# The query products of a decoder's first attention layer on operands of 512 columns, with the halves added on VectorE

## What is computed

```python
h = rmsnorm(x, mixer_norm[0])
parts = split_cols(h @ even_w_in[0], [ATTN_W] * N_DIL + [ATTN_W, ATTN_W, CROSS_WIDTH])
mix = mixer_dilated(parts[:N_DIL], parts[N_DIL], parts[N_DIL + 1], rel_bias)
...
def mixer_dilated(q_groups, k, v, rel_bias):
    branches = [dilated_branch(heads(qg), kh, vh, rel_bias, w, d)
                for qg, (w, d) in zip(q_groups, DIL_PAIRS)]
    m_max = jnp.max(jnp.stack([b[1] for b in branches]), axis=0)
    ...
    return (num / den[..., None]).astype(k.dtype).reshape(B, S, ATTN_W)
```

## Time and profile before

| | |
|---|---|
| median of 3 runs | 1565.93 us (1565.57 to 1566.80) |
| the profiled execution, its own time | 1565.14 us |
| its span in the trace | 1563.4 us |
| mean granted clock of TensorE | 0.993 |
| TensorE busy | 1527.9 us (98%), 8155 matmuls |
| VectorE busy | 1326.0 us (85%) |
| ScalarE busy | 1130.7 us (72%) |
| the chain that ended last, by engine | TensorE 89%, VectorE 4%, ScalarE 3%, DMA 2% |

### The profile page before, as it was taken

The page is one execution under the profiler, slowest core; times in us unless marked ns, Lnnn a source line. Parts: engine busy times, 40 slices in busy tenths (PEclk is TensorE's granted clock), DMA queues, the critical chain, the costliest instruction groups (busy, mean ns, idle before and its releaser), DMA issues.

```text
span 1563.4 us, 25330 instructions
## 1 busy us (share of the span) xinstructions
PE 1527.9 (98%) x8155; PEld 1288.0 (82%) x8155; DVE 1326.0 (85%) x1806; ACT 1130.7 (72%) x1507; POOL 87.7 (6%) x64
## 2 busy tenths in 40 slices
PE   8899999999999999999999999999999999999997
PEld 7899977888888777888888888888888888888886
DVE  5778868777758878998998998998998998998997
ACT  5565556444446668788878878878878878878875
POOL 1333100000010000000000000000000000000000
PEclk9999999999999999999999999999999999999999
DMA  9844526666623467999999999999999999999992
GB/s 271 216 135 142 159 91 201 189 187 184 167 58 85 145 250 285 409 386 375 381 396 357 396 390 355 393 389 354 390 394 354 388 392 356 392 393 349 404 386 107
DMA packets 226997, 455.38 MB, mean 291 GB/s; under 512 B 12848, under 2 KB 120512, under 8 KB 226944
## 3 DMA queue, kind: packets, MB, share of 16 engines
q1 hardware_dynamic: 222800, 439.52, 77.7%
q0 software_dynamic: 4144, 15.22, 3.9%
HBM read 445.52 MB, written 9.18 MB: 291 GB/s over the span
## 4 chain that ended last, share of the span: by engine, by line
PE 89%; DVE 4%; ACT 3%; DMA 2%; issue 1%; POOL 0%; ACTq 0%; DVEq 0%; POOLq 0%
PE ps L733 25%; PE ps L735 25%; PE ps L734 25%; PE ps L980 5%; PE ps L982 2%; PE ps L1140 2%; DMA big<-in_even_w_in 2%; PE ps L821 1%; ACT w_hi L1178 1%; PE ps L851 1%; DVE w_lo L1525 1%; DVE small L1612 1%; PE ps L836 1%; DVE z L1590 1%; DVE z L1609 1%
## 5 line engine op out<-in xcount | busy, mean ns | idle before, releaser
L1525 DVE TENSOR_TENSOR w_lo<-big,w_hi 128x1024 fp32r<-128x1024 f32 x837 | 983.8, 1214 | 145.2 <-ACT w_hi L1178 69.6
L1438 ACT CAST w_hi<-big 128x1024 fp32r<-128x1024 f32 x672 | 693.6, 1056 | 139.6 <-PE ps L735 136.5
L733 PE MATMUL ps<-w_hi,m_hi 128*128 128x512 f32 (+1 forms) x1008 | 391.9, 389 | 1.5 <-ACT qT L1233 1.3
L735 PE MATMUL ps<-w_hi,m_lo 128*128 128x512 f32 (+1 forms) x1008 | 389.4, 386 | 0.0
L734 PE MATMUL ps<-w_lo,m_hi 128*128 128x512 f32 (+1 forms) x1008 | 389.2, 386 | 0.0
L733 PEld LDWEIGHTS ps<-w_hi,m_hi 128*128 128x128 f32 x1008 | 189.7, 188 | 41.2 <-issue 2.1
L735 PEld LDWEIGHTS ps<-w_hi,m_lo 128*128 128x128 f32 x1008 | 189.6, 188 | 38.3
L734 PEld LDWEIGHTS ps<-w_lo,m_hi 128*128 128x128 f32 x1008 | 189.7, 188 | 37.2
L1178 ACT CAST w_hi<-big 128x1024 fp32r<-128x1024 f32 (+1 forms) x171 | 165.9, 981 | 49.3 <-PE ps L735 36.8
L733 PE MATMUL ps<-w_hi,h_two 128*128 128x512 f32 (+1 forms) x464 | 182.6, 394 | 0.0
L735 PE MATMUL ps<-w_hi,h_two 128*128 128x512 f32 (+1 forms) x464 | 179.9, 388 | 0.0
(11 more groups left out here) (270 smaller groups left out, 1576.0 us busy)
## 6 DMA issues: line engine op xcount, KB each, us to landing
big<-in_odd_w_gate SPq DMA_DIRECT2D x112, 1024.0 KB, 7.3
big<-in_odd_w_up SPq DMA_DIRECT2D x112, 1024.0 KB, 7.4
big<-in_odd_w_down SPq DMA_DIRECT2D x112, 1024.0 KB, 7.5
big<-in_even_w_in SPq DMA_DIRECT2D x42, 512.0 KB, 4.0
big<-in_even_w_gate SPq DMA_DIRECT2D x22, 512.0 KB, 4.6
big<-in_even_w_up SPq DMA_DIRECT2D x22, 512.0 KB, 3.9
big<-in_even_w_down SPq DMA_DIRECT2D x22, 512.0 KB, 4.7
big<-in_w_out SPq DMA_DIRECT2D x20, 512.0 KB, 3.6
```

What stands on the lines that cost most here:

```text
L733: mm(dst, a[0], b[0], start=start, stop=False, **kw)
L735: return mm(dst, a[1], b[0], start=False, stop=stop, **kw)
L1438: nc.scalar.copy(w_hi[:, slot, :], ring[s][:, (u % 2) * UNIT:(u % 2 + 1) * UNIT]).then_inc(s_hi, 1)
L1525: return V.tensor_tensor(dst, src, lead.bitcast(F32), ALU.subtract)
```

## The change

The 24 query products (m < NBR in the first layer) become wide products. For each chunk one matmul of 512 columns takes the weights' high part by the tokens' high and low parts together, and one of 256 adds the weights' low part by the tokens' high part to the first half. The function for it, `wide_product`, is the dense layer's code taken out, and the dense layer now calls it. Keys, values and the cross pairs stay as they were. The bank then holds two halves that have to be added: ScalarE copies the second half into `half`, a view of the tile XH with two places, and raises `query_half_copied`; VectorE adds it to the first half in PSUM, writes qT and raises `evacuated` (`halves`). `evacuated` of layer 0 counts query products alone now; keys, values and the cross pairs' queries have semaphores of their own. A product's wait for its bank is therefore for VectorE's add where the bank held queries (`even_bank`), and the scores wait for the keys' copy and for the third add. On VectorE an add stands ahead of the first split, of the second split and of the third split in a step, and at the start of the stage behind pair 0's five splits.

```diff
@@ -372,6 +372,7 @@
         ysb = z[:, 0:D]
+        half = XH[:, 0, 0:2 * SEQ].rearrange("p (r n) -> p r n", r=2)
         fin_gain = qiT[:, :, :].rearrange("p c n -> p (c n)")
@@ -407,10 +408,11 @@
         s_hi, s_lo, s_used = map(sem, ("unit_hi", "unit_lo", "unit_used"))
-        names = ("evacuated", "turned_v", "values", "scores", "scores_read", "masked", "max", "exp",
+        names = ("evacuated", "cross_queries", "turned_v", "values", "scores", "scores_read", "masked", "max", "exp",
                  "added", "summed", "third_left", "third_read", "probs", "probs_turned", "probsT", "mixed", "mix_hi", "mix_lo", "dve_rden")
...
         s_me = sem("mem_evacuated")
+        s_two, s_keyT, s_valT = map(sem, ("query_half_copied", "even_keys_copied", "even_values_copied"))
         s_plo = sem("unit_lo_by_pool")
@@ -501,6 +503,10 @@
 
+        def wide_before(pair, m):
+            return pair.value(lambda g: NBR * g + m)
         def width(pair, m):
@@ -778,10 +784,39 @@
 
+            def wide_product(dst, w, norm=None):
+                for k in range(DC):
+                    if norm is not None:
+                        pe.wait_ge(s_nlo, DC * norm + k + 1)
+                    mm(dst, w[0][:, k, :], h_two[:, k, :, :].rearrange("p s n -> p (s n)"),
+                       start=k == 0, stop=k == DC - 1, skip_group_check=True)
+                    last = mm(dst[:, 0:SEQ], w[1][:, k, :], h_hi[:, k, :], start=False, stop=k == DC - 1,
+                              skip_group_check=True)
+                last.then_inc(s_used, 1)
+            def even_bank(pair, m):
+                if m == 0:
+                    pe.wait_ge(s_keyT, pair.g)
+                elif m == 1:
+                    pe.wait_ge(s_valT, pair.g)
+                else:
+                    pe.wait_ge(s_at[0]["evacuated"], wide_before(pair, m - 2) + 1)
             def project(pair, m, norm=None):
...
                 n = pair.before() + m
-                if not (isinstance(n, int) and n < 2):
+                if pair.kind == "even":
+                    if not (isinstance(n, int) and n < 2):
+                        even_bank(pair, m)
+                elif pair.cross and pair.l == 0:
+                    pe.wait_ge(S["evacuated"], NBR * PAIRS)
+                    pe.wait_ge(s_keyT, PAIRS)
+                    pe.wait_ge(s_valT, PAIRS)
+                elif pair.cross:
+                    pe.wait_ge(S["evacuated"], 3 * PAIRS)
+                elif not (isinstance(n, int) and n < 2):
                     pe.wait_ge(S["evacuated"], n - 1)
@@ -789,11 +824,17 @@
                 w = split(pair.idx, pair.span[0], pair.unit(m), kc, width(pair, m))
+                if pair.kind == "even" and m < pair.nbr:
+                    wide_product(ps[:, pair.bank(m), :], w, norm)
+                    return
                 product(ps[:, pair.bank(m), 0:SEQ], w, src, kc, norm)
...
                 S = s_at[pair.l]
-                pe.wait_ge(S["evacuated"], pair.before() + pair.mats)
+                if pair.kind == "even":
+                    pe.wait_ge(s_valT, pair.g + 1)
+                else:
+                    pe.wait_ge(S["evacuated"], pair.before() + pair.mats)
                 for t in range(TT):
@@ -804,7 +845,13 @@
                 S = s_at[pair.l]
-                pe.wait_ge(S["evacuated"], pair.before() + (1 if pair.cross else pair.nbr + 1))
+                if pair.cross:
+                    pe.wait_ge(S["cross_queries"], pair.g - PAIRS + 1)
+                elif pair.kind == "even":
+                    pe.wait_ge(s_keyT, pair.g + 1)
+                    pe.wait_ge(S["evacuated"], wide_before(pair, NBR - 1) + 1)
+                else:
+                    pe.wait_ge(S["evacuated"], pair.before() + pair.nbr + 1)
 
@@ -856,7 +903,7 @@
                 if ch == 0:
-                    pe.wait_ge(s_at[l]["evacuated"], pair_at(l, NPAIR - 1).before() + 1)
+                    pe.wait_ge(s_at[l]["cross_queries"], XPAIRS)
                     pe.wait_ge(s_at[l]["scores_read"], 2 * PAIRS + 1)
@@ -974,14 +1021,7 @@
                 bank = (4 if kind == "gate" else 6) + par
-                for k in range(DC):
-                    if norm is not None:
-                        pe.wait_ge(s_nlo, DC * norm + k + 1)
-                    mm(ps[:, bank, :], w[0][:, k, :], h_two[:, k, :, :].rearrange("p s n -> p (s n)"),
-                       start=k == 0, stop=k == DC - 1, skip_group_check=True)
-                    last = mm(ps[:, bank, 0:SEQ], w[1][:, k, :], h_hi[:, k, :], start=False, stop=k == DC - 1,
-                              skip_group_check=True)
-                last.then_inc(s_used, 1)
+                wide_product(ps[:, bank, :], w, norm)
 
@@ -1223,6 +1263,12 @@
                 act.wait_ge(s_used, along(pair.idx, pair.span[0], [u + 1 for u in pair.unit(m)]))
+                if pair.kind == "even" and m < pair.nbr:
+                    n = wide_before(pair, m)
+                    if not (isinstance(n, int) and n < 2):
+                        act.wait_ge(S["evacuated"], n - 1)
+                    nc.scalar.copy(half[:, (pair.par + m) % 2, :], ps[:, pair.bank(m), SEQ:2 * SEQ]).then_inc(s_two, 1)
+                    return
                 if pair.gs[0] == NPAIR - 1:
@@ -1230,7 +1276,11 @@
                 dst = qT[:, pair.par, m, :] if m < pair.nbr else kT[:, pair.par, :] if m == pair.nbr else vT[:, :]
-                nc.scalar.copy(dst, ps[:, pair.bank(m), 0:SEQ]).then_inc(S["evacuated"], 1)
+                if pair.kind == "even":
+                    done = s_keyT if m == pair.nbr else s_valT
+                else:
+                    done = S["cross_queries" if pair.cross else "evacuated"]
+                nc.scalar.copy(dst, ps[:, pair.bank(m), 0:SEQ]).then_inc(done, 1)
 
@@ -1612,6 +1662,15 @@
 
+            def halves(pair, m):
+                S = s_at[0]
+                dve.wait_ge(s_two, wide_before(pair, m) + 1)
+                if not (isinstance(pair.g, int) and pair.g < 2):
+                    dve.wait_ge(S["mixed"], 2 * pair.g - 1)
+                V.tensor_tensor(qT[:, pair.par, m, :], half[:, (pair.par + m) % 2, :], ps[:, pair.bank(m), 0:SEQ],
+                                ALU.add).then_inc(S["evacuated"], 1)
             def head_probs(pair, hh):
@@ -1643,10 +1702,16 @@
                     outs(lo_now, now, m)
+                def add(m):
+                    if now.gs[-1] < LATE:
+                        halves(nxt, m)
                 if now.kind == "even":
+                    add(0)
                     low(0)
+                    add(1)
                     low(1)
                     head_probs(now, 1)
+                    add(2)
                     low(2)
@@ -1678,7 +1743,10 @@
                         lo_mat(pair_at(l, 0), m)
+                    halves(pair_at(l, 0), 0)
                     for m in range(pair_at(l, 1).mats):
+                        if m + 1 < NBR:
+                            halves(pair_at(l, 0), m + 1)
                         lo_mat(pair_at(l, 1), m)
```

## The result

The changed kernel takes 1571.28 us (median of 7 runs, 1570.07 to 1574.53) beside 1565.93 for the kernel before in the same comparison (7 runs, 1565.16 to 1567.1). The ratio is **1.0043, with a 95% interval of 1.0033 to 1.0052**: slower by 0.43%. The forecast was 1568.7, at most 1570.5, and "same" as the likeliest.

What follows compares the result with a forecast made beforehand. TensorE's pace of starting matmuls was taken as the bound. Stall +2.73, clock +1.35, first step +0.06 and -0.07, six further steps -1.26 sum to +2.8 us: 1565.93 becomes 1568.7, range 1566.0 to 1570.5.

Steps and rivals of the forecast that it cites:

- What bounds the kernel: First layer's attention: TensorE's pace of starting matmuls sets the time; VectorE has some 7 us free in 40.
- Part 1, the wide products: First layer's 24 query products: fewer matmul starts gain 0.07 us a product, -1.26 us over six loop steps.
- The rival of the weight loads: Query products: time falls with their weight loads, 0.96 us a product, giving 1546.9 us; chance 0.02.
- Part 2, the adds: VectorE's 24 adds of 0.42 us: nothing lost in the loop's further steps, +0.06 us in the first step.
- Part 3, the stall: Stage start: pair 0's product 2 waits for add 0 behind the fifth unit's split, +2.80 us, net +2.73.
- Part 4, the clock: Stage start: after the new 2.85 us idle time TensorE's clock falls once more, +1.35 us (bounds 0 and 1.36).
- The slower rival: Loop: scores wait for add 2, so the steps' gains are lost; +4.2 us, 1570.1 us; 0.16 for slower in all.
- The range: Whole kernel: 1566.0 to 1570.5 us, leaving out no stall, weight loads and a tip of the slower case.

Runs made afterwards that it cites:

- experiment 2: The changed kernel with GpSimd's mask sums in the loop also waiting for the fourth split of their step: 1567.86 us, 1.0018.
- experiment 1: The changed kernel with a step's third add ahead of the second head's probabilities, not behind them: 1570.06 us, 1.0028.
- experiments 3 and 6: experiment 3, and the kernel before with only GpSimd's mask sums waiting for the fourth split of their step: 1564.32 us, 0.9990.
- experiment 9: The kernel before with ScalarE's copy of pair 0's product 0 also waiting for pair 0's last split: 1569.5 us, 1.0026.
- experiment 5: The changed kernel with 12 matmuls that nothing reads ahead of pair 0's product 2: 1571.42 us, 1.0036.
- experiment 3: The kernel before with an unused 0.41 us VectorE maximum between second probabilities and third split in each step: 1569.86 us, 1.0031.
- the cures: The changed kernel with GpSimd's sums behind the fourth split, and with copies and adds interleaved among pair 0's casts and splits: together 1565.51 us, 0.9997.

## Why the prediction was wrong

- **What bounds the kernel: right for the kernel before, and it held only there.** VectorE's "some 7 us free in 40" was an average. It did not lie behind the probabilities, where the price arose.
- **Part 1, the wide products: right for the product, half for the loop.** Query products have a chunk pitch of 0.35 (131.27, 131.62 in a step), and 0.08 a product comes out where TensorE sets the pace (experiment 2's last steps). The term was to be 1.26 in the loop; with the splits cured, the profiles show 0.7 to 0.8 over six steps, since in the middle steps TensorE waits a little for other engines. The rival of the weight loads is gone: a third fewer loads for these products, and nothing like 23 us. The busy share of the weight loads fell from 37.41 of 40 to 33.30, and the stage became longer. What the prediction's rival drew from "Perfetto Trace Analysis" of the Trainium skill (Identifying the Most-Contended Engine) is an inference that goes further than the page: it names the matmuls' share of peak work beside the busy share of the weight loads, as measures of headroom, and does not say that a product's time falls with its loads.
- **Part 2, the adds: their duration right (0.41 against 0.42), the step behind add 2 wrong.** This is the step that failed: "Behind add 2 VectorE's next split is 0.4 us later, and the one after it waits for a cast that ends later still, so the reading of the scores does not move." I moved the split and left its duration at 1.22. It became 2.29, the next one 2.2, and the reading moved by 1.4 us a step. The sentence after it, "GpSimd waits for the probabilities, not for the adds", was true, and was the cause: GpSimd's start stayed where it was while the split moved behind it. The prediction had no term for VectorE's splits in the loop, and in place of -1.26 the steps gave +2.58, an error of 3.8 us, which is more than the sum that was forecast. The earlier trace rows showed splits of 2.3 us beside mask sums, and I used it for the start alone; the earlier trace rows showed a sum of 2.27 that had waited, the other half of the same contest.
- **Part 3, the stall: the mechanism right, the size right where product 1 starts as before.** There (experiment 1) product 2 comes 2.83 us later (2.80 forecast). In the changed kernel's own profile the wait is 5.63 long, because product 1 was early, and product 2 starts 1.22 us later than before. What the prediction left out is that an early product 1 makes a wait ahead of product 2 in the kernel before as well: 3.83 and 4.30 us in the profiles of experiments 3 and 6. The stall is longer with the add, not new.
- **Part 4, the clock: not as forecast.** A second fall, on top of the one before product 1, was to cost 1.35. Only experiment 1 has two (behind 47.99 and behind 54.98), and there the parts add up: 2.83 for the stall and 1.57 for product 2 at the lower clock make the 4.39 by which its first keys come late; 4.1 was forecast. The changed kernel's own profile has one fall, as the kernel before has, only a product later: it costs product 2 2.05 us and product 1 nothing, and the first keys come 3.26 later. That the start as a whole lost about what was forecast (3.2 us by the means above, 0.26% in experiment 9) owes something to luck: three of four profiles with the start of before have a fall too, and the second fall that was forecast came in one of three with the changed start. That the clock is part of the loss over many executions is not shown (experiment 5).
- **The slower rival** had 0.16 and the wrong mechanism: no scores waited for add 2. In the changed kernel's step they are released by the keys' copy, as forecast. Its time, 1570.1, was the nearest, by chance.
- **The range** (to 1570.5) missed the median by 0.8 us. Its bounds were those of the terms that I had; a bound for a split that turns slow (1.07 us more each, two a step, against the earlier trace rows) was missing. Its chance of "slower", 0.22, was to be 0.16 and 0.07, which is 0.23; nothing hangs on it.

Left open: why the loss of 0.31% in experiment 3 is larger than the 2.6 us of its steps. Its profile has a fall of the clock at the end of the stage as well (51.41 us for 49.81); with a start 0.6 us later the three make up the 4.9 us by which its span is longer. Where this place was left as it is, the clock fell in five of seven profiles with wide products and in one of four with narrow ones, this one, and it cost 1.6 to 3.1 us (51.36 to 52.89 for 49.8). Whether late VectorE work makes that fall more likely, or chance did, one profile a kernel can't tell. So part of the change's 0.43% may lie there too; the cures leave little room for it, since with both of them the ratio is 0.9997 and that kernel's profile has the fall as well (52.89).

## What to carry to other kernels

Before putting a short operation on an engine, look at who is released by the instruction ahead of it. If another engine's work starts there and contends with the instruction behind, the insertion hands over the first place: 0.41 us cost a split of 1.22 another 1.07, twice a step, though the engine had slack on average. What cured it here is one wait that keeps the engine without urgency (here GpSimd, idle 14 us a step) behind the urgent one. And at the start of a stage count where in a queue of long operations the new one stands, not how long it takes.

## What the runs showed of the hardware

- **Two engines that hold each other off over SBUF.** A split (two operands and a result in SBUF) takes 1.22 us alone and 2.1 to 2.3 beside GpSimd's sums; a sum takes 1.27 when it comes first, 2.08 when it comes second to a split, 1294 ns on average when kept apart. VectorE's 128x256 operations that read PSUM are not held: the reading at 123.23 took 0.41 while GpSimd was in its sums (118.75 to 124.5). The page "SBUF — State Buffer" of the Trainium skill, named above, says that a VectorE operation with two SBUF inputs is concerned where GpSimd's operation reads SBUF, and that whoever starts first has the ports for the whole instruction. The traces agree: the engine that came second took about 0.8 to 1.1 us longer. Here a lead of 0.05 us was enough to be first (118.75 against 118.80, and 115.89 against 115.94 in experiment 3).
- **The same idle time, and two outcomes for the clock.** 2.41 and 2.42 us before the same matmul, at 1.00 behind one and 0.50 behind the other, with no difference in the program there. Such falls made 1.6 to 3.1 us between single executions at the end of the stage and 1.8 at the second layer's start, so a difference of profiles of that size is no evidence until a second kernel repeats it.
